# Another order of VectorE's instructions within a head of an mLSTM kernel

## What is computed

```python
proj = x @ w_in                                   # columns xm, z, o_pre (and two gates)
xc = silu(causal_dwconv(xm, conv_w, conv_b))      # 4 taps along the tokens
q = xc @ w_q * DK ** -0.5;  k = xc @ w_k;  v = xm @ w_v
h = mlstm_chunkwise(q, k, v, i_pre, log_sigmoid(f_pre))   # 8 chunks of 128 tokens
hn = normalise(h) * norm_g
hb = sigmoid(o_pre) * hn + skip * xc
out = (hb * silu(z)) @ w_out                      # over all heads
```

## Time and profile before

| | |
|---|---|
| median of 3 runs | 1647.09 (1644.94 to 1647.63) |
| the profiled execution: its own time | 1649.82 |
| its span (first to last instruction) | 1648.0 |
| mean granted TensorE clock in the span | 0.963 of full speed |
| PE busy | 1544.8 (94%) |
| DVE busy | 1027.3 (62%) |
| ACT busy | 570.3 (35%) |
| POOL busy | 204.1 (12%) |

### The profile page before, as it was taken

One profiled execution on the slowest core, in us unless ns is written; L12 is line 12 of the kernel. 1 busy time (PEld: TensorE's weight loads), 2 busy tenths in 40 slices (PEclk: granted clock), 3 DMA queues, 4 the chain that ended last, 5 costly groups with the idle time before them and its releaser, 6 DMA issues.

```text
span 1648.0 us, 20245 instructions
## 1 busy us (share of the span) xinstructions
PE 1544.8 (94%) x6994; PEld 1277.2 (78%) x6994; DVE 1027.3 (62%) x1557; ACT 570.3 (35%) x878; POOL 204.1 (12%) x161
## 2 busy tenths in 40 slices
PE   7998989989899898998999999989999999989998
PEld 5887777878778787787888888867887777768886
DVE  4865676566765667656674413367777787769324
ACT  4632423324233242331543423455333333343210
POOL 3312122021220212203210000000000000000001
PEclk9999999999999999999999999989999999989999
DMA  5112112121021211202155333342222221174121
GB/s 169 53 33 81 41 26 78 33 80 38 25 85 29 76 38 29 86 25 76 45 208 179 111 86 105 91 141 63 75 88 78 87 74 56 50 281 128 39 90 51
DMA packets 113965, 133.14 MB, mean 81 GB/s; under 512 B 7128, under 2 KB 89192, under 8 KB 113392
## 3 DMA queue, kind: packets, MB, share of 16 engines
q1 hardware_dynamic: 112832, 132.28, 25.3%
q10 hardware_dynamic: 1072, 0.07, 0.0%
HBM read 102.93 MB, written 29.39 MB: 80 GB/s over the span
## 4 chain that ended last, share of the span: by engine, by line
PE 75%; DVE 18%; ACT 4%; issue 2%; DMA 1%; DVEq 0%; POOL 0%; ACTq 0%; SPq 0%; POOLq 0%
PE wide L1849 19%; PE wide L1850 18%; PE wide L1851 18%; DVE tmp_a L1363 4%; PE ps_intra L1972 2%; PE ps_inter L1975 1%; PE ps_state L1977 1%; DVE tmp_a L1358 1%; DVE blk L1613 1%; PE ps_s L1849 1%; DVE f_buf L1402 1%; PE ps_s L1851 1%; PE ps_intra L1851 1%; PE ps_s L1850 1%; PE ps_intra L1849 1%
## 5 line engine op out<-in xcount | busy, mean ns | idle before, releaser
L1849 PE MATMUL wide<-x_hi,w_hi 128*128 128x512 f32 x768 | 312.4, 407 | 42.6 <-DVE tmp_c L1343 42.6
L1851 PE MATMUL wide<-x_hi,w_lo 128*128 128x512 f32 x768 | 303.2, 395 | 0.0
L1850 PE MATMUL wide<-x_lo,w_hi 128*128 128x512 f32 x768 | 302.8, 394 | 0.0
L1849 PEld LDWEIGHTS wide<-x_hi,w_hi 128*128 128x128 f32 x768 | 147.3, 192 | 72.3 <-issue 44.0
L855 POOL TENSOR_TENSOR w_lo<-w_raw,w_hi 128x1024 fp32r<-128x1024 f32 x48 | 127.7, 2661 | 354.6 <-ACT w_hi L932 353.5
L1851 PEld LDWEIGHTS wide<-x_hi,w_lo 128*128 128x128 f32 x768 | 146.6, 191 | 32.2
L1850 PEld LDWEIGHTS wide<-x_lo,w_hi 128*128 128x128 f32 x768 | 147.6, 192 | 28.7
L1850 PE MATMUL wide<-xa,blk 128*128 128x512 f32 x384 | 149.9, 390 | 0.0
L1849 PE MATMUL wide<-xb,blk 128*128 128x512 f32 x320 | 129.0, 403 | 15.1 <-DVE zz L1684 14.3
L1851 PE MATMUL wide<-xb,blk 128*128 128x512 f32 x320 | 127.4, 398 | 0.0
L893 POOL TENSOR_SCALAR small<-small 128x1 f32<-128x1 f32 x15 | 4.1, 272 | 734.9 <-ACT gate_b L1103 485.6
(11 more groups left out here) (320 smaller groups left out, 3408.4 us busy)
## 6 DMA issues: line engine op xcount, KB each, us to landing
w_raw<-in_mlstm_w_in SPq DMA_DIRECT2D x48, 512.0 KB, 3.8
y_heads<-f_buf SPq DMA_DIRECT2D x32, 256.0 KB, 2.0
wu_raw<-in_pool_w_u SPq DMA_DIRECT2D x32, 256.0 KB, 2.8
wm_raw<-in_mlstm_w_out SPq DMA_DIRECT2D x16, 512.0 KB, 5.4
folded<-stage SPq DMA_DIRECT2D x32, 256.0 KB, 2.8
a_raw<-in_pool_w_z SPq DMA_DIRECT2D x16, 512.0 KB, 3.4
a_raw<-folded SPq DMA_DIRECT2D x16, 512.0 KB, 3.6
y_rows<-zz SPq DMA_DIRECT2D x16, 512.0 KB, 2.6
```

Source lines behind the costliest of these rows:

```text
L1849: pe.matmul(dst, a[0], b[0], start=first, stop=False, skip_group_check=more)
L1850: pe.matmul(dst, a[0], b[1], start=False, stop=False, skip_group_check=more)
L1851: return pe.matmul(dst, a[1], b[0], start=False, stop=last, skip_group_check=more)
```

## The change

The work is the same, instruction for instruction; only DVE's order within a head changes, with the waits that stand in front of the moved instructions.

- In heads 1 to 7 `gated_output` of the head behind is put ahead of the whole first convolution, where it stood behind three of its taps.
- The section behind the convolutions is put in another order. Before: per half of z, the gate product (L1398), with f = skip * xc and `xc_lo` behind halves 0 and 2, f * e behind halves 1 and 3, and the first half of `xm_lo` behind half 2. After: f of tile 0, `xc_lo` of tile 0, gate product 0, f of tile 1, `xc_lo` of tile 1, gate product 1, gate product 2, the first half of `xm_lo`, gate product 3, both f * e, the second half of `xm_lo`.
- The wait for the stores of the head behind (`y_head_out`) stands ahead of all of these, where it stood behind the first gate product.

```diff
-                    for f in work[:3]:
-                        f()
                     gated_output(h - 1, uses, [at["hn"] + m for m in range(4)])
-                    for f in work[3:]:
+                    for f in work:
                         f()
...
-                for m in range(4):
+                def gate_z(m):
                     k, j, n = at["z"] + m, m // 2, m % 2
                     dve.wait_ge(z_tanh, h * 4 + (m + 1))
                     link_taken(dve, dve.scalar_tensor_tensor(
                         out=e_buf[:, j, half(n)], in0=gate_t[:, m % 2, :], scalar=1.0, in1=bank(k),
                         op0=ALU.add, op1=ALU.mult), uses, k)
-                    if n:
-                        step(dve.tensor_tensor(f_buf[:, j, :], f_buf[:, j, :], e_buf[:, j, :], ALU.mult))
-                    else:
-                        if not first and m == 0:
-                            dve.wait_ge(y_head_out, h * 64)
-                        step(dve.tensor_scalar(f_buf[:, j, :], xc[:, j, :], col(h * 2 + (COL_SKIP + j)), None, ALU.mult))
-                        dve.wait_ge(xc_high, h * 2 + (j + 1))
-                        link(dve, dve.tensor_tensor(xc_lo[:, j, :], xc[:, j, :], xc_hi[:, j, :].bitcast(F32),
-                                                    ALU.subtract), xc_low, h * 2 + (j + 1))
-                    if m == 2:
-                        low_xm(0)
+
+                def low_xc(j):
+                    dve.wait_ge(xc_high, h * 2 + (j + 1))
+                    link(dve, dve.tensor_tensor(xc_lo[:, j, :], xc[:, j, :], xc_hi[:, j, :].bitcast(F32),
+                                                ALU.subtract), xc_low, h * 2 + (j + 1))
+
+                if not first:
+                    dve.wait_ge(y_head_out, h * 64)
+                for j in range(2):
+                    step(dve.tensor_scalar(f_buf[:, j, :], xc[:, j, :], col(h * 2 + (COL_SKIP + j)), None, ALU.mult))
+                    low_xc(j)
+                    gate_z(j)
+                gate_z(2)
+                low_xm(0)
+                gate_z(3)
+                for j in range(2):
+                    step(dve.tensor_tensor(f_buf[:, j, :], f_buf[:, j, :], e_buf[:, j, :], ALU.mult))
                 low_xm(1)
```

## The result

The changed kernel takes 1564.47 (median of 4 runs, 1562.89 to 1568.25) against 1646.49 for the kernel before on the same chip: ratio 0.9506, 95% interval 0.9486 to 0.9526. The forecast was 1574 in a range of 1567 to 1590. The profiled execution took 1562.89, its span is 1561.1 and its mean clock 0.993 (before: 0.963).

A forecast was written before the change was run, and what follows sets the result against it. PE, busy 94% of the span, was taken as the bound, so its waits pay. 42.6 + 11.2 + 13.0 + 10.2 - 4.2 = 72.8 off the profiled 1649.82 gave 1577.0, as median 1574; range 1567 to 1590.

The forecast's parts named there:

- Parts 1 and 2: Behind the turns in heads 1 to 7: PE's wait for L1343 goes, 42.6, and the half clock behind it, 11.2.
- The rival that the clock falls anyway behind the turns: At `xm1`, half clock follows the transposes even without a wait; gain only 61.6, time 1586; chance 9%.
- The opening: At 21.0 to 28.7, almost only transposes with the clock at 1.00; taken as evidence for full clock through the turns.
- Part 3: Convolution moved behind the gated output stays covered by ACT's later tanh: margin 1.3 to 3.7, cost nothing.
- Part 4: SP's stores are issued about 6.5 earlier; DVE's wait stands some 20 after the last issue; cost nothing.
- Parts 5 and 6: At q, PE's wait for the second `xc_lo` goes, 13.0, and half clock behind it in heads 1 to 6, 10.2.
- part 5: Behind the second `xc` gate, low parts ahead of gate products: `xc_lo` 1 ends at 384.0, wanted at 384.8; gain 13.0.
- part 7: At v, a late `xm_lo` makes new waiting for PE: 0.6 a head, 4.2 in all, bounds 0 and 10.5.
- the work behind the heads keeps its length: After PE's end of head 7, the remaining work starts earlier but takes as long as before.
- the rivals: Clock falls 9%, wait for `xc_lo` stays 10%, convolution becomes the bound 5%, slower 3%, change does not reach the wait 3%.
- the wait at q: Rival: PE's wait for `xc_lo` stays through a POOL hold-up or late `xc_hi`; gain 53.8, time 1593; chance 10%.

The follow-up runs named there:

- The first half alone: Kernel before with only the gated output put ahead of all convolution taps, low parts and gate products in the old order: 1588.1, ratio 0.9646.
- the two runs with extra taps: Changed kernel with three or two more executions of tap 0 between gated output and convolution: 1575.4 and 1573.2.
- The second half alone: Changed kernel with gated output behind three taps again, keeping low parts ahead of gate products and f * e behind them: 1622.7, ratio 0.9848.
- the second set: Second group of four kernels measured beside the kernel before, among them the unmodified changed kernel again: 1563.5 against 1645.2.
- the shifted kernels: Kernel before with one, two, three or four added sets of full-width matmuls right behind the heads: 1646.5, 1645.1, 1647.8, 1642.6 against 1647.3.

## Why the prediction was right and where it was wrong

**Parts 1 and 2** (the first wait and the clock behind it, 53.8): right. The bank is free at 318.21, `xm1` starts behind the last transpose, and the clock is 1.00 there. The first half alone brought 56.0, a little more because the clock was up at q in most heads. The rival that the clock falls anyway behind the turns is refuted: 1.91 of transposes between matmuls of full width leave 1.00 granted. The opening, on which the prediction leaned, was weaker evidence than it took it for: in the kernel before the clock is 0.50 from 28.80 to 32.00, right behind that stretch and a wait of 1.61 at its end, and in the changed kernel it is 1.00 at the same work (28.00 to 31.20).

The Trainium skill (TensorE: Matmul & The Clock Gate, section Part 4: PE-mode transpose) says that full clock does not engage for transposes. What the prediction drew from it, that `xm1` would start at the lower level, did not come; whether transposes by themselves would raise the clock, no run here shows.

**Part 3**: right in kind and size. The margin was put at 1.3 to 3.7 and is 2.14, and the two runs with extra taps show that work beyond it is paid for, the more so where it runs into POOL's splits.

**Part 4**: right; DVE does not wait for the stores.

**Parts 5 and 6** (23.2): right. The second half alone brought 21.7. f of tile 1 was held up as forecast (2.14, ending 0.55 behind the split at 349.26), and the margin at q is 0.71 where 0.8 was forecast. But of the moves that part 5 lists, that of f * e alone was enough; the low parts could have stayed behind the gate products. In head 3 the parts add up: 6.20 + 1.6 + 1.97 + 1.7, less 0.23 of new waiting (part 7), is 11.24, and the head is 11.26 shorter.

**Part 7** is a term that was mis-sized: 0.6 of new waiting a head, 4.2 in all. Measured in head 3 are 0.14 at the first half of v and 0.09 at the second (353.64 to 354.01 and 359.54 to 359.86, where 0.23 lies between matmuls), 0.23 a head, 1.6 in all. The second `xm_lo` was put 0.5 behind PE's need and came 0.1 behind it. The sum of the heads was 72.8 and is 76.9; 2.6 of the difference is this term.

**The step that failed** is the sentence that the work behind the heads keeps its length, and with it the low end of the range, which took only the 2 to 3 of scatter that three runs of before had shown. That stretch takes 798.6 to 806.4 with the same work, with the clock that follows its waits. With the gain of the heads alone the time would have been 1569.6 (1646.49 - 76.9), inside the range. The other 5.1 lie in that stretch and in the opening (93.6 to 98.5); in the profiled pair they gave 7.8 and 2.2.

The 5.1 came again as 4.9 in the second set, so most of it seems to go with the change and not with chance, though the second profile of the changed kernel has 805.5 behind the heads. How it does so is open: the shifted kernels speak for the place of the later work, but no run had the changed kernel's later work in the old place.

None of the rivals came; the wait at q had been given 10%.

## What to carry to other kernels

When the bounding engine waits for a buffer, look at what stands ahead of the instruction that frees it in the other engine's program: here 6.2 a head hung on taps of a convolution that ACT took up only 8.7 after the last of them (356.78 to 365.51). Idle time in front of an instruction is margin only after the time of the step that ends the wait is taken off it, and work that moves later into it can meet another engine's (here 6.06 for 4.14). And when a change takes waits away, give the range room for the clock in stages that the change does not touch.

## What the runs showed of the hardware that was not expected

- The same wait of PE, 1.97 at q, was followed by half clock in all six heads of the loop in the kernel before and in two of the six when the wait ahead of it was gone. One of 2.94 for `zz` was followed by half clock in one profile of the changed kernel and not in the other. A wait of 1.25 behind transposes left the clock at 1.00.
- 2.73 of added matmuls made a kernel 4.7 faster (0.9976 [0.9959, 0.9994]).
- In head 3, instructions of DVE of 512 or 1024 columns that read only SBUF and met a running split of POOL ended 0.5 to 1.1 behind its end (0.55 for f, 0.55 for the addition of 512 columns, 1.07 for the tap of the earlier trace rows); the products that read PSUM and one tile of SBUF (L1343, L1396) kept their 0.75 and 0.69 beside it.
